# A decoder step in one program: the openings of prologue and attention reworked, and another order on the vector engine inside attention

## What is computed

```
h = rms_norm(x);  z = h @ w_in            # u_val, u_gate, q, k, v, qi, ki, wi
u = u_val * sigmoid(u_gate)
conv = silu(layer_norm(depthwise_conv31(u) + b))
q, k = rope(rms_norm(q)), rope(rms_norm(k))          # 8 query heads, 4 key heads of 64
score[t,s] = sum_h wi[t,h] * relu(qi[t,h] . ki[s])   # 16 index heads
sel = the 256 best admissible keys of each row by score
attn = softmax(q . k[sel] / 8) @ v[sel]              # sample rows: cached pages + new keys
x = x + concat(conv, attn) @ w_out
x = x + (silu(h2 @ w_gate) * (h2 @ w_up)) @ w_down   # h2 = rms_norm(x)
```

## Time and profile before

| | |
|---|---|
| the three runs | 1668.42, 1669.55, 1670.69 us, median 1669.55 |
| the profiled execution | 1669.33 us, of which 1667.5 us span |
| busy | PE 92%, DVE 54%, POOL 33%, ACT 26% |
| prologue up to the first product of the key block | 0 to 29 us |
| projections, u, taps, index scores | 29 to 332 us |
| selection, with k, v and q beside it | 332 to 424 us |
| between selection and attention | 424 to 475 us |
| attention loop | 475 to 759 us |
| output projection and FFN | 759 to 1667.5 us |

### The profile page before, as it was taken

How to read it: one execution, slowest core, us unless ns; L and a number is a source line. 1 busy time by engine, 2 the same in 40 slices (tenths; PEclk the granted TensorE clock), 3 DMA queues, 4 the chain that set the end, 5 groups by cost and what they waited for, 6 DMA issues and landing times.

```text
span 1667.5 us, 24356 instructions
## 1 busy us (share of the span) xinstructions
PE 1537.3 (92%) x9069; PEld 1412.7 (85%) x9069; DVE 896.5 (54%) x1568; ACT 428.1 (26%) x786; POOL 545.4 (33%) x438
## 2 busy tenths in 40 slices
PE   4999988889956787899999999999999999999999
PEld 3998767548735676689999999999999999999999
DVE  6799889999756775444352433324243341423323
ACT  3200258755244544452131010010100001010000
POOL 3643211131358500014424333243433425343320
PEclk9999999999977888889999999999999999999999
DMA  6212100120243232014211111111111111111102
GB/s 203 83 39 79 56 13 27 39 64 26 83 157 96 77 108 77 2 63 164 71 39 39 39 51 38 38 50 36 52 38 50 40 35 50 50 38 50 38 0 107
DMA packets 68638, 100.17 MB, mean 60 GB/s; under 512 B 12017, under 2 KB 49137, under 8 KB 68431
## 3 DMA queue, kind: packets, MB, share of 16 engines
q1 hardware_dynamic: 63714, 94.32, 17.9%
q10 hardware_dynamic: 4853, 4.93, 0.9%
HBM read 86.57 MB, written 13.02 MB: 60 GB/s over the span
## 4 chain that ended last, share of the span: by engine, by line
PE 69%; DVE 17%; issue 6%; ACT 4%; DMA 2%; POOL 1%; SPq 0%; DVEq 0%; ACTq 0%; POOLq 0%
PE ps L906 20%; PE ps L908 19%; PE ps L907 19%; DVE y_e L2007 2%; PE ps L1222 2%; DVE mcnt L2128 2%; PE ps L1210 1%; DVE y L2007 1%; PE ps L1194 1%; ACT rl L1596 1%; ACT lo_t L1730 1%; PE ps L1195 1%; PE ps L1350 1%; DMA xt<-in_x_t 1%; DVE sm L2305 1%
## 5 line engine op out<-in xcount | busy, mean ns | idle before, releaser
L906 PE MATMUL ps<-hi_t,w_hi 128*128 128x384 f32 (+2 forms) x1464 | 479.9, 328 | 6.6 <-DVE lo_t L1923 3.9
L908 PE MATMUL ps<-hi_t,w_lo 128*128 128x384 f32 (+2 forms) x1464 | 478.6, 327 | 0.0
L907 PE MATMUL ps<-lo_t,w_hi 128*128 128x384 f32 (+2 forms) x1464 | 478.2, 327 | 0.0
L906 PEld LDWEIGHTS ps<-hi_t,w_hi 128*128 128x128 f32 (+1 forms) x1464 | 274.7, 188 | 9.2 <-POOL w_lo L753 2.9
L907 PEld LDWEIGHTS ps<-lo_t,w_hi 128*128 128x128 f32 (+1 forms) x1464 | 274.8, 188 | 0.5
L908 PEld LDWEIGHTS ps<-hi_t,w_lo 128*128 128x128 f32 (+1 forms) x1464 | 274.6, 188 | 0.6
L2534 DVE TENSOR_TENSOR x<-x,ps 128x384 f32<-128x384 f32 (+1 forms) x264 | 139.2, 530 | 105.4 <-PE ps L908 104.6
L906 PE MATMUL ps<-f_hi,w_hi 128*128 128x384 f32 (+1 forms) x528 | 175.1, 332 | 2.9 <-DVE x L2534 2.5
L907 PE MATMUL ps<-f_lo,w_hi 128*128 128x384 f32 (+1 forms) x528 | 172.6, 327 | 0.0
L908 PE MATMUL ps<-f_hi,w_lo 128*128 128x384 f32 (+1 forms) x528 | 172.5, 327 | 0.0
L889 POOL CAST w_hi<-w_raw 128x1024 fp32r<-128x1024 f32 x60 | 62.8, 1047 | 334.1 <-PE ps L908 334.1
(11 more groups left out here) (317 smaller groups left out, 2391.9 us busy)
## 6 DMA issues: line engine op xcount, KB each, us to landing
w_raw<-in_w_gate SPq DMA_DIRECT2D x22, 512.0 KB, 3.4
w_raw<-in_w_up SPq DMA_DIRECT2D x22, 512.0 KB, 3.4
w_raw<-in_w_down SPq DMA_DIRECT2D x22, 512.0 KB, 3.4
w_raw<-in_w_in SPq DMA_DIRECT2D x16, 512.0 KB, 3.6
kt_b<-in_cache_kt SPq DMA_DIRECT2D x48, 128.0 KB, 2.3
v_b<-in_cache_v SPq DMA_DIRECT2D x48, 128.0 KB, 2.5
x<-in_x_t SPq DMA_DIRECT2D x8, 544.0 KB, 8.0
w_raw<-in_w_u SPq DMA_DIRECT2D x8, 512.0 KB, 3.7
```

The costliest lines, as they stand in the source:

```text
L906: pe.matmul(out, a_hi, b_hi, start=first, stop=False)
L907: pe.matmul(out, a_hi, b_lo, start=False, stop=False)
L908: return pe.matmul(out, a_lo, b_hi, start=False, stop=last)
```

## The change

The prologue's casts of the first two weight units go from POOL to ACT, PE spreads the scales of block 0 before it sums block 1, and DVE takes the means of block 1 after four scalings of block 0. Between selection and attention the flag test and the small masks go ahead of the keys' norm; the sample rows' queries are handled before tile 7's, both have late places, and tile 7's queries and the low and high parts of the last 128 keys go into the first turns of the attention loop, where the first scores now wait for the first 896 keys only. In the loop DVE masks the scores first and takes low parts behind that, divides the finished tile before the taps, takes no taps at n < 2 and at n % 8 == 7, and the sample values move to n = 16, 32, 47, 63.

```diff
+VALUES_AT = (16, 32, 47, 63)
-LATE_QUERY = NT - 1
+NORMS = ALL[1:-1] + [SAMPLE, S // P - 1]
+LATE_QUERY = NT - 2
@@ places of the late queries
-        qst_late = at_w("qst_late", 28672, [SR, NH * HD])
-        hsq_late = at_w("hsq_late", 38912, [SR, NH * HD])
+        qst_late = at_w("qst_late", 28672, [P, 2, NH * HD])
+        hsq_late = at_w("hsq_late", 38912, [P, 2, NH * HD])
@@ POOL
-                pool.tensor_copy(w_hi[:, n % SLOTS, 0:w], w_raw[:, n % RAW, 0:w]).then_inc(split_hi, 1)
+                if n > 1:
+                    pool.tensor_copy(w_hi[:, n % SLOTS, 0:w], w_raw[:, n % RAW, 0:w]).then_inc(split_hi, 1)
...
+                if b == 0:
+                    pool.wait_ge(q_zero, 2)
+                    query_inverses(LATE_QUERY)
+                    pool.wait_ge(head_rs, LATE_QUERY + 2)
             pool.wait_ge(q_zero, 4)
-            query_inverses(LATE_QUERY)
+            query_inverses(LATE_QUERY + 1)
@@ PE
             rows_sums(0)
+            spread_scales(0)
             rows_sums(1)
-            spread_scales(0)
...
-                    pe.wait_ge(kt_ready, 2 * NKV)
-                    pe.wait_ge(kt_lo, 2 * NKV)
+                    pe.wait_ge(kt_ready, NKV)
+                    pe.wait_ge(kt_lo, NKV)
...
-                if n - 7 in SAMPLE_AT:
-                    sample_values(SAMPLE_AT.index(n - 7))
-                if n - 9 in SAMPLE_AT:
-                    sample_outputs(SAMPLE_AT.index(n - 9))
+                if n in VALUES_AT:
+                    sample_values(VALUES_AT.index(n))
+                if n - 2 in VALUES_AT:
+                    sample_outputs(VALUES_AT.index(n - 2))
@@ ACT
+            def cast_unit(n):
+
+                w = D if n > 0 else KT * KIW
+                act.wait_ge(raw_in[n % RAW], 16)
+                act.activation(w_hi[:, n, 0:w], w_raw[:, n, 0:w], ACT.Copy).then_inc(split_hi, 1)
+
             square_rows(0)
+            cast_unit(0)
             square_rows(1)
+            cast_unit(1)
...
             take_keys(0, S - P)
-            take_query(S // P - 1)
-            store_query(S // P - 2)
-            take_keys(S - P, S)
+            store_query(LATE_QUERY - 1)
+            take_query(LATE_QUERY + 1)
...
-            store_query(S // P - 1)
             take_query(LATE_QUERY)
+            square_query(LATE_QUERY)
...
+                if n == 0:
+                    square_query(LATE_QUERY + 1)
+                if n == 1:
+                    take_keys(S - P, S)
                 if n == 2:
                     store_query(LATE_QUERY)
+                if n == 4:
+                    store_query(LATE_QUERY + 1)
@@ DVE, prologue
-            row_means(1)
             for j in range(NB):
                 norm_tiles(j, 0, 4)
+                if j == 0:
+                    row_means(1)
@@ DVE: the flag test, its branch and the small masks, from behind the query tiles
@@ to ahead of dve.wait_ge(head_rs, 1), and
-            for o in range(S // P - 1):
+            for o in range(LATE_QUERY):
                 query_squares(o)
                 query_rotation(o)
...
             key_lows(0, S - P, 0)
-            query_squares(S // P - 1)
-            query_rotation(S // P - 1)
-            key_lows(S - P, S, NKV)
...
-            weight = [n // NH + 1 if n < CONV_HEADS else 0 for n in range(NA)]
+            weight = [n // NH + 1 if 2 <= n < CONV_HEADS and n % NH != 7 else 0 for n in range(NA)]
@@ DVE, attention loop
             for n in range(NA + 4):
-                if n % NH == 5 and n > NH + 1:
-                    lows(n // NH - 1)
-                if n % NH == 7 and n < NA - NH and n - 1 not in LN_AT:
-                    query_lows(n // NH + 1)
...
                 if n < NA:
                     mask_scores(n)
+                if n % NH == 5 and n > NH + 1:
+                    lows(n // NH - 1)
                 if n >= 2 and n - 2 < NA:
                     take_weights(n - 2)
+                if n % NH == 7 and n < NA - NH and n - 1 not in LN_AT:
+                    query_lows(n // NH + 1)
+                if n % NH == 2 and n > NH:
+                    outputs(n // NH - 1)
...
+                if n == 2:
+                    key_lows(S - P, S, NKV + 1)
+                if n == 3:
+                    query_squares(LATE_QUERY + 1)
+                    query_rotation(LATE_QUERY + 1)
...
-                if n - 8 in SAMPLE_AT:
-                    sample_rows(SAMPLE_AT.index(n - 8))
-                if n % NH == 2 and n > NH:
-                    outputs(n // NH - 1)
+                if n - 1 in VALUES_AT:
+                    sample_rows(VALUES_AT.index(n - 1))
```

More of the change, by code:

```diff
@@ L1229, in output_transposes @@
                 n = NH * (i + 1) + 3
-                begun, ended = sum(at < n for at in SAMPLE_AT), sum(at + 9 < n for at in SAMPLE_AT)
+                begun, ended = sum(at < n for at in SAMPLE_AT), sum(at + 2 < n for at in VALUES_AT)
                 if begun > 0:
@@ L1246, in layer_norm_sum @@
                 pe.wait_ge(spt_ready, 2 * sum(at + 1 <= n for at in SAMPLE_AT))
-                pe.wait_ge(so_ready, sum(at + 7 <= n for at in SAMPLE_AT))
-                pe.wait_ge(sot_ready, sum(at + 9 <= n for at in SAMPLE_AT))
+                pe.wait_ge(so_ready, sum(at <= n for at in VALUES_AT))
+                pe.wait_ge(sot_ready, sum(at + 2 <= n for at in VALUES_AT))
                 if v == 0:
@@ L1680, in take_query, with square_query @@
                 ins.then_inc(proj_evac, 1)
-                act.wait_ge(proj_evac, BASE[4] + o + 1)
+            def square_query(o):
+                qs, squares = query_tile(o)
+                act.wait_ge(proj_evac, BASE[4] + TILES.index(NORMS[o]) + 1)
                 if 2 <= o < LATE_QUERY:
@@ L1699, in take_keys @@
                                        scale=kf[half, K_GQC:K_GQC + 1]).then_inc(kt_ready, 1)
-            take_query(0)
-            take_query(1)
+            for o in range(2):
+                take_query(o)
+                square_query(o)
             act.wait_ge(k_ready, 1)
@@ L1708, in _ @@
             store_query(0)
-            for o in range(2, S // P - 1):
+            for o in range(2, LATE_QUERY):
                 take_query(o)
+                square_query(o)
                 store_query(o - 1)
@@ L2181, in _ @@
             link(ins)
+            dve.wait_ge(flag_in, 16)
+            link(dve.reduce_max(s_row[:, P:P + 1], s_row[:, 0:P], AX_X))
+            link(dve.tensor_copy(s_flag[:, :], s_row[:, P:P + 1]))
+            again = dve.value_load(s_flag[0:1, 0:1], min_val=0, max_val=1)
+            with dve.If(again > 0):
+                base = 0
+                for k in range(NSEL + 1):
+                    work, place, r = select_tile(k)
+                    with dve.Fori(0, TOPK // 8) as i:
+                        dve.max(m8[0:r, :], work).then_inc(round_done, 1)
+                        dve.wait_ge(round_done, 2 * i + (base + 1))
+                        dve.sem_inc(fence_dve, 1)
+                        dve.match_replace(work, m8[0:r, :], work, TAKEN).then_inc(round_done, 1)
+                        dve.wait_ge(round_done, 2 * i + (base + 2))
+                    base += 2 * (TOPK // 8) + 1
+                    dve.tensor_scalar(place, work, TAKEN, DROP, ALU.not_equal, ALU.mult).then_inc(round_done, 1)
+                dve.wait_ge(round_done, base)
+            for t in range(FIRST):
+                if t > 0:
+                    dve.memset(mneg[:, mask_at(t):mask_at(t) + t * P], 0.0)
+                dve.tensor_copy(mneg[:, mask_at(t) + t * P:mask_at(t + 1)], kb[:, 0:P]).then_inc(masks_ready, 1)
+            link(dve.tensor_tensor(smx[:, :].rearrange("p (b t) -> p b t", b=NS),
+                                   kb[0:SR, P + NS * SR:].rearrange("p (b t) -> p b t", b=NS),
+                                   smneg[:, PAST:].unsqueeze(1).broadcast_to([SR, NS, TS]), ALU.min))
+            dve.sem_inc(masks_ready, 1)
             dve.wait_ge(head_rs, 1)
```

59 lines of the change are left out of this document (18 added, 41 removed).

## The result

The changed kernel took 1639.51 us (median of 4 runs, 1635.14 to 1641.87) beside 1668.99 us for the kernel before, measured with it: a ratio of 0.9827, 95% interval 0.9804 to 0.9849. The forecast was 1646.0 us, range 1637.5 to 1658.0: right in sign, inside the range, 6.5 us too high. The profiled execution took 1637.19 us.

A forecast was written before the change was run, and what follows sets the result against it. It took PE to bound prologue and end, mutual waits the opening, and DVE nearly the loop; 2.5 + 11.5 + 9.5 = 23.5 us saved gave 1646.0 us, range 1637.5 to 1658.

The forecast's parts named there:

- Part A: Prologue: scaling starts 2.8 us earlier and the key block ends sooner; 2.5 us saved, ends 0 and 4.
- the two cases: Prologue: key block's last wait ends 1.8 us earlier if low parts stand behind POOL's subtraction, 3.4 if not.
- Part B: Opening of attention: flag test hidden, first mask and sample rows earlier, no tap wait; 11.5 us saved, bounds 8 and 13.
- Step (2): Opening: low parts follow ACT's key copies, tile 7 and last keys leave the path; first mask 3.25 us earlier.
- Part C: Attention loop: DVE's new order removes waits of DVE and PE; 9.5 us saved, ends 3 and 16.
- n = 53 and 61: Loop: masks leave the 5 us waits; 0 at n=53, where PE needs the same low parts, 1.0 us at 61.
- the queries' low parts: Loop: mask ahead of them lets mask and taps fill DVE's wait; 2.0 us at n=23, 3.2 at n=39.
- the division: Loop: placed before the taps, PE's values no longer wait; 1.2, 1.1 and 1.4 us in tiles 1, 2 and 5.
- the loop gives nothing: Rival, loop: DVE waits after a mask instead of before; only 14.0 us saved overall, 1655.5 us, chance 0.20.
- My second rival: Rival, loop: far more waits go and PE's clock falls less; 1634 us, chance 0.15.
- The slower rival: Rival, loop at n=7, 15, 23, 31, 39: low parts delayed behind masks and scores; 1674 us at d = 5, chance 0.04.
- The absorbed gain: Rival, output projection: loads of w_out or x fix its start, so nothing is gained; 1669.5 us, chance 0.03.

The follow-up runs named there:

- after_again: The changed kernel with no edit, profiled once more: 1638.94 us, ratio 0.9831 to the kernel before.
- flag_old: The changed kernel with flag test and small masks back behind the rotations, ahead of the keys' low parts: 1642.55 us, ratio 0.9843 to the kernel before.
- loop_old: The changed kernel with DVE's old loop order (low parts ahead of masks, division behind taps): 1653.81 us, ratio 0.9918 to the kernel before.
- lows61: The changed kernel with the outputs' low parts ahead of the mask again at n=61 only: 1645.16 us, ratio 0.9869 to the kernel before.
- ln_behind: The changed kernel with heads' scores and masks also moved ahead of the layer norm's sums and steps: 1636.42 us, ratio 0.9798 to the kernel before.
- ln_filled: As ln_behind, but PE computes the scores of n=47 four times and of n=55 three times: 1633.13 us, ratio 0.9795 to the kernel before.
- query_lows_old: The changed kernel with the queries' low parts ahead of the mask again: 1638.85 us, ratio 0.9814 to the kernel before.

## Why the prediction was right, and where its steps were not

**Reading.** That the engines waited for each other in the opening and that the end moves with the loop's end was right: the projection moved by 31.2 us, the end by 32.1.

**Part A**, 2.5 us: 3.4 at the key block, 0.95 at the end of the selection in the first pair; about 3 by the medians of the traces, which is not shown clear of their spread. The scaling began 3.5 us earlier, not 2.8, as block 0's diagonal lay ready at 17.81 us (16.87 + 0.94), not at 19.23. Of the two cases the better came, because POOL's subtraction began at 24.83, behind DVE's first low part. That it travels on unchanged was wrong for a single execution: with the new prologue the selection's end lies up to 11 us apart. Up to 5 us of that are the stalls beside POOL, and 9.7 us are there already when the selection's first operation on one element per partition starts (359.87 to 369.54 us); the fall of the clock near 230 us, in after and not in after_again, is one source of these.

**Part B**, 11.5 us: 13.6 in the pair of profiles (13.1 with the repeat). The mechanism held at each step; the first mask came 0.7 us and the sample rows 1.9 us better than the sum. What was wrong is the sentence that the flag test "without that cover would cost 2.56". Step (2) itself had DVE stand for ACT's query copies, from 467.4 to 469.6; the wait was 1.79 us, and flag_old shows that it takes up most of the flag test and leaves 0.9. The sample rows' chain, 9.8 us by my sum, came at 12.6 (481.18 for 493.82), 0.95 of it from the selection's shift. SP's loads began at 463.77, 4.6 us before my 468.4, and cost nothing, as the tap was asked for at 476.36.

**Part C**, 9.5 us: 16.7 in the first pair, 12.9 to 13.4 with the other three traces of the same code. Up to n=60 I had 8.5, the traces give 7 to 11. After n=60 I had 1.0, and it was 5.9. That is the term that was mis-sized, "n = 53 and 61: the masks leave the 5 us waits ... at 61 it doesn't (1.0)": I priced the wait (1.2 us as measured) and not the clock behind it. Of the 6.5 us by which the forecast missed, 5 are this one place. Inside the 8.5 the split was off: the queries' low parts, 5.2 us in my sum, give about 1; the division, 3.7, gives 3 to 4.5; the sample values at n=16 and 32, 0, aren't told from 0. These come to 4 to 5.5 us of the 7 to 11; the rest belongs to the order too, by loop_old, but no run splits it further. So that the sum up to n=60 came out near 8.5 is in part luck: a term of 5.2 us was too large by 4, and gains that I had not listed took its place.

**Rivals.** That the loop gives nothing is refuted by loop_old. My second rival, more waits gone and the clock no longer falling, names what made the difference, but spread it as a seventh of a mean over the loop. Most of it sits in a place: at n=61 one wait decides over up to 10 us of work at half speed. The slower rival's price did not show: the time fell. The absorbed gain is out.

## What to carry to other kernels

Price a wait of PE together with the clock behind it: look at the granted clock and at the durations of the same products in the stretch behind the wait, and ask whether what follows is PE-bound. Where it is, a wait of 1.8 us can cost 6, as at n=61. Put what feeds PE's next product ahead of whatever waits for a third engine, and try it one place at a time: moving the mask ahead of low parts was worth 5 to 6 us at n=61 and about 1 at n=39. And profile the unchanged kernel twice before you explain a difference of 4 us between two traces.

## What the runs showed of the hardware

- The clock fell to 0.50 behind an idle time of PE of only 1.83 us. In lows61 and before it stayed there for about 10 us of unbroken work of PE, in loop_old for about 3.5. Between n=48 and n=52 such a fall made the same heads take 20.2 to 20.3 us in eight traces, 23.45 in three and 21.8 in one (ln_behind and ln_filled have another order there).
- Work that nobody needs made the needed products faster: 2.82 us in place of 5.46, with a clock of 1.00 in place of 0.83 from 620 to 640 us (ln_filled and ln_behind).
- DVE's operations of one column, 0.16 us, took up to 2.37 us beside POOL's cast or subtraction of 128x1024, to the end of it. DVE's maximum beside the same cast kept its time (0.69 us at 397.19 in the kernel before, the cast from 397.34 to 398.38). In the selection these stalls add up to 0.2 us in query_lows_old and 5.2 in the kernel after; the other traces lie between.
